# adaLN products on unsplit fp32 weights, four 512-column strips in the array's four column groups, with 8 KB rows per load

## What is computed

```python
def adaln(c, w, b):
    mod = jax.nn.silu(c) @ w + b                 # (sequences, 2048) @ (2048, 6144)
    shift, scale, gate = jnp.split(mod[:, None, :], 3, axis=-1)
    return shift, scale, gate

for l in range(2):                               # 0: windowed attention, 1: mLSTM
    h = rmsnorm(x, g_pre[l]) * (1.0 + scale) + shift
    y = branch_l(h)                              # in-projection, mixer, SiLU gate, out-projection
    x = x + gate * rmsnorm(y, g_post[l])
```

## Time and profile before

| | |
|---|---|
| median of 3 runs | 2599.01 us (2595.3 to 2606.03) |
| span of the profiled execution | 2596.8 us |
| PE busy | 2449.3 us, 94% |
| weight loads of PE (beside its matmuls) | 2259.8 us, 87% |
| VectorE busy | 1213.0 us, 47% |
| ScalarE busy | 875.6 us, 34% |
| mean granted TensorE clock | 0.951 of 2.4 GHz |
| DMA, mean over the span | 116 GB/s |
| loads of w_ada | 32 of 1 MB in ada0, 128 of 0.5 MB in out0 and out1 |

### The profile page before, as it was taken

One profiled execution on the slowest core, in us unless ns is written; L12 is line 12 of the kernel. 1 busy time (PEld: TensorE's weight loads), 2 busy tenths in 40 slices (PEclk: granted clock), 3 DMA queues, 4 the chain that ended last, 5 costly groups with the idle time before them and its releaser, 6 DMA issues.

```text
span 2596.8 us, 42451 instructions
## 1 busy us (share of the span) xinstructions
PE 2449.3 (94%) x17089; PEld 2259.8 (87%) x17089; DVE 1213.0 (47%) x1739; ACT 875.6 (34%) x1303; POOL 65.2 (3%) x108
## 2 busy tenths in 40 slices
PE   5979999999999899999699999999999999989996
PEld 4679989889898598888499999999999999988996
DVE  6663453543544645553943343333343434355424
ACT  5732342332432445553431222121212222234322
POOL 1000000000000000000000000000000000000000
PEclk9989999999999599999899989899999999989998
DMA  8863222222121047777254966774649556616731
GB/s 324 306 211 94 76 55 64 71 66 85 50 68 49 1 151 234 238 242 223 76 111 68 83 85 96 68 98 74 98 66 88 95 88 76 96 50 211 247 81 69
DMA packets 346795, 300.84 MB, mean 116 GB/s; under 512 B 9585, under 2 KB 288361, under 8 KB 345497
## 3 DMA queue, kind: packets, MB, share of 16 engines
q1 hardware_dynamic: 336976, 247.88, 44.9%
q0 software_dynamic: 9360, 50.19, 5.3%
q10 hardware_dynamic: 290, 0.27, 0.0%
HBM read 274.81 MB, written 27.56 MB: 116 GB/s over the span
## 4 chain that ended last, share of the span: by engine, by line
PE 82%; DMA 7%; DVE 5%; ACT 3%; issue 2%; DVEq 1%; ACTq 0%; SPq 0%
PE PJ L746 57%; DMA arena<-in_w_ada 3%; PE MX L938 3%; PE MX L864 3%; PE MX L885 3%; DMA raw<-in_w_in_mlstm 3%; PE PJ L711 2%; PE MX L871 2%; PE MX L1060 1%; PE MX L1070 1%; DMA raw<-in_w_in_attn 1%; PE MX L828 1%; PE MX L1022 1%; DVE strips L1788 1%; DMA obuf<-in_w_ada 1%
## 5 line engine op out<-in xcount | busy, mean ns | idle before, releaser
L746 PE MATMUL PJ<-h_hi,w_hi 128*128 128x272 f32 x4384 | 944.3, 297 | 39.0 <-DVE h_lo L1579 24.7
L746 PE MATMUL PJ<-h_hi,w_lo 128*128 128x272 f32 x4384 | 922.1, 292 | 0.0
L746 PE MATMUL PJ<-h_lo,w_hi 128*128 128x272 f32 x4384 | 920.9, 292 | 0.1
L746 PEld LDWEIGHTS PJ<-h_hi,w_hi 128*128 128x128 f32 x4384 | 713.8, 193 | 73.6 <-issue 38.6
L746 PEld LDWEIGHTS PJ<-h_lo,w_hi 128*128 128x128 f32 x4384 | 705.8, 193 | 0.0
L746 PEld LDWEIGHTS PJ<-h_hi,w_lo 128*128 128x128 f32 x4384 | 701.3, 193 | 0.2 <-issue 0.2
L1521 DVE TENSOR_TENSOR w_lo<-raw,w_hi 128x2048 fp32r<-128x2048 f32 x106 | 242.9, 2292 | 406.5 <-ACT w_hi L1159 406.4
L1159 ACT ACTIVATE w_hi<-raw 128x2048 fp32r<-128x2048 f32 x106 | 202.0, 1905 | 42.1 <-DMA raw<-in_w_in_mlstm 34.6
L1788 DVE TENSOR_TENSOR strips<-arena,strips 128x1024 fp32r<-128x1024 f32 x128 | 153.1, 1223 | 82.2 <-ACT strips L1349 80.4
L1349 ACT ACTIVATE strips<-arena 128x1024 fp32r<-128x1024 f32 x128 | 131.4, 1060 | 107.9 <-DMA arena<-in_w_ada 107.5
L938 PE MATMUL MX<-strips,cT 128*128 128x512 f32 x512 | 141.9, 399 | 17.9 <-DVE strips L1788 17.9
(11 more groups left out here) (303 smaller groups left out, 2137.1 us busy)
## 6 DMA issues: line engine op xcount, KB each, us to landing
arena<-in_w_ada SPq DMA_DIRECT2D x128, 512.0 KB, 5.0
raw<-in_w_in_mlstm SPq DMA_DIRECT2D x64, 1024.0 KB, 14.8
raw<-in_w_in_attn SPq DMA_DIRECT2D x40, 1024.0 KB, 5.6
obuf<-in_w_ada SPq DMA_DIRECT2D x32, 1024.0 KB, 7.8
raw<-in_w_out_attn SPq DMA_DIRECT2D x16, 1024.0 KB, 7.8
raw<-in_w_out_mlstm SPq DMA_DIRECT2D x16, 1024.0 KB, 6.5
x_spill<-arena POOLq DMA_DIRECT2D x2, 4352.0 KB, 12.3
arena<-x_spill POOLq DMA_DIRECT2D x2, 4352.0 KB, 17.7
```

Source lines behind the costliest of these rows:

```text
L746: last = mm(PJ[:, 2 * pair + f, 0:HT], w, h[:, k, HT * f:HT * f + HT], start=(k == 0 and n == 0), stop=(k == KT - 1 and n == 2))
```

## The change

- Nothing of the adaLN weights is split any more. A step takes 128 rows x 2048 columns in full fp32: four products with the same 32 columns of c (nine real ones and the next row block's or padding), each 512 moving columns into 32 partitions of one PSUM bank, thus into its own quarter of the array's columns (`ada_step`). Six quads of 2048 columns take 16 steps each, instead of 24 groups.
- Loads are 1 MB with rows of 8 KB, in four buffers: obuf in the first stage, the arena later.
- First stage: no phase of its own in the table of weight units. 32 steps alternate between shift and scale, PE waits only for the load, and a buffer is free after its step. The turns of x lie behind steps 2, 4, ..., 10 and one row block of square sums behind each of steps 14 to 29. SP no longer waits for c.
- out0 and out1: four steps per block, behind row blocks 4, 7, 10 and 13, in the same blocks as before. SP issues the four loads of block k-1 ahead of the weight of block k.
- A finished quad (4 x 32 partitions x 512) is copied by ScalarE and turned by four 128 x 128 transposes, in the next block behind row block 3; VectorE adds the bias, which is loaded once at the start (bvec, a fourth small load that `vec_in` waits for) and turned with the norm weights. POOL issues no bias loads and waits for no group: its spill of x waits for the turned x only.
- The loops of out0 and out1 over pairs of blocks are written out.

```diff
-OWNER = dict(A="d", Z="d", O="d", Q="a", K="a", V="a", Y="a", G="a")
+OWNER = dict(Z="d", O="d", Q="a", K="a", V="a", Y="a", G="a")
 L0K = "VQQQQKZZZZ"
 L1K = "QKVVZOZO"
-PHASES = [("ada0", 1, "A" * 8), ("l0", GR, L0K), ("out0", 1, "Y" * KT), ("gate", 1, "G"),
-          ("l1", MH, L1K), ("out1", 1, "Y" * KT)]
+PHASES = [("l0", GR, L0K), ("out0", 1, "Y" * KT), ("gate", 1, "G"), ("l1", MH, L1K), ("out1", 1, "Y" * KT)]
 
...
-SEGS = dict(out0=[(0, 2, None), (2, 4, (0, 2 * D, 8)), (6, 8, (1, 0, 12))],
-            out1=[(0, 2, None), (2, 4, (1, 2 * D, 20)), (6, 8, None)])
-SQ_PARTS = {(5, 3): range(0, 4), (5, 7): range(4, 8), (6, 3): range(8, 12), (6, 7): range(12, KT)}
-STRIPS = 8
-RING = 4
+ADA = 4
+QUADS = dict(out0=(2, 3, 4), out1=(5,))
+STEPS = {"out0": {2 + s // 4: range(4 * (s // 4), 4 * (s // 4) + 4) for s in range(0, 48, 4)},
+         "out1": {2 + s // 4: range(48 + 4 * (s // 4), 48 + 4 * (s // 4) + 4) for s in range(0, 16, 4)}}
+QCOL = {2: (0, 2 * D), 3: (1, 0), 4: (1, D), 5: (1, 2 * D)}
+X_TURN = {2: 0, 4: 1, 6: 2, 8: 3, 10: 4}
+SQ_AT = {14 + k: k for k in range(KT)}
...
-            sp.wait_ge(c_in, 32)
-            for u in range(32):
-                if u >= 4:
-                    sp.wait_ge(lo_done, 2 * (u - 3))
-                if u == 28:
+            for u in range(2 * KT):
+                if u >= ADA:
+                    sp.wait_ge(a0_used, u - ADA + 1)
+                if u == 2 * KT - 2:
 
                     sp.wait_ge(xt_done, 5)
                     for e in range(2):
                         load_entry((None, 0), e)
-                slot = obuf[:, 4 * (u % 4):4 * (u % 4) + 4, 0:512]
-                sp.dma_start(slot, ada[:, 0, 4 * (u % 4):4 * (u % 4) + 4,
-                                       512 * (u // 4):512 * (u // 4) + 512]).then_inc(a0_in[u % 4], 16)
+                sp.dma_start(a0_raw[u % ADA], ada[:, 0, u // 2, D * (u % 2):D * (u % 2) + D]).then_inc(a0_in[u % ADA], 16)
...
+                for k in range(1, KT + 1):
+                    if k - 1 in STEPS[ph]:
+                        for s in STEPS[ph][k - 1]:
+                            l, col = QCOL[2 + s // KT]
+                            if s == STEPS[ph][2][0]:
+                                for se, v in arena_free:
+                                    sp.wait_ge(se, v)
+                            if s >= ADA:
+                                sp.wait_ge(u_used, s - ADA + 1)
+                            sp.dma_start(u_raw[s % ADA], ada[:, l, s % KT, col:col + D]).then_inc(u_in[s % ADA], 16)
+                    if k < KT:
+                        load(ph, (None, 0), k, 0, w[:, :, P * k:P * k + P])
...
-            out_units("out0", wout[0], [(kv_stored, 32 + 64 * GR)])
+            out_units("out0", wout[0], [(kv_stored, 32 + 64 * GR), (om_done, 1 + 18 * GR)])
-                if t:
-                    bias(t - 1, t == 1)
-                bias(a)
-            bias(8)
-            pool.wait_ge(u_used, RING + 12 * STRIPS)
+            pool.wait_ge(u_used, 3 * KT)
-                bias(a)
...
-            def ada_products(ph, it, e, mid=None):
-
-                pair = pair_of(ph, e)
-                for j in range(8):
-                    s = j // 2 % 2
-                    pe.wait_ge(lo_done, unit_no(ph, it, e, j) + 1)
-                    for k in range(2):
-                        lhsT = cT[:, (2 * j + k) * 18:(2 * j + k) * 18 + P]
-                        at = SW * (j % 2) + k * 512
-                        for w in (w_hi, w_lo):
-                            last = mm(PJ[:, 2 * pair, :], lhsT, w[s][:, at:at + 512],
-                                      start=(j == 0 and k == 0 and w is w_hi),
-                                      stop=(j == 7 and k == 1 and w is w_lo))
-                    last.then_inc(w_used, 1)
-                    if mid:
-                        mid(j)
-
-            def ada_turn(ph, it, e, n):
-
-                pair = pair_of(ph, e)
-                pe.wait_ge(mod_copied, n + 1)
-                pe.wait_ge(bias_in, n * 16 + 16)
+            def ada_step(bank, weights, k):
+
+                lhsT = cT[:, NSEQ * k:NSEQ * k + 32]
+                for g in range(4):
+                    last = mm(bank[32 * g:32 * g + 32, :], lhsT, weights[:, 512 * g:512 * g + 512],
+                              start=(k == 0), stop=(k == KT - 1))
+                return last
+
+            def ada_turn(bank, rows_):
                 for j in range(4):
-                    last = mm(PJ[:, 2 * pair + 1, 9 * j:9 * j + 9], misc[32:51, P * j:P * j + P],
-                              fix[32:51, C_SEL:C_SEL + NSEQ], start=True, stop=True)
+                    last = tr(bank[:, P * j:P * j + P], rows_[:, P * j:P * j + P], ident)
                 last.then_inc(mod_turned, 1)
...
+            for u in range(2 * KT):
+                pe.wait_ge(a0_in[u % ADA], 16 * (u // ADA + 1))
+                ada_step(PJ[:, u % 2, :], a0_raw[u % ADA], u // 2).then_inc(a0_used, 1)
+                if u in X_TURN:
+                    turn_x(X_TURN[u])
+                if u in SQ_AT:
+                    sums(0, [SQ_AT[u]])
+            for q in range(2):
+                pe.wait_ge(mod_copied, q + 1)
+                ada_turn(PJ[:, 2 + q, :], mod_rows[q])
...
-            def strip(n, j):
-
-                at = fixed(pe, n + 1)
+            def strip(s):
+
                 pe.wait_ge(ct_ready, 1)
-                pe.wait_ge(u_lo_done, at)
-                for k in range(2):
-                    lhsT = cT[:, (2 * j + k) * 18:(2 * j + k) * 18 + P]
-                    for w in (u_hi, u_lo):
-                        last = mm(MX[:, 2, :], lhsT, w[j % RING][:, k * 512:k * 512 + 512],
-                                  start=(j == 0 and k == 0 and w is u_hi),
-                                  stop=(j == STRIPS - 1 and k == 1 and w is u_lo))
-                last.then_inc(u_used, 1)
-
-            def turn_group(n):
-
-                pe.wait_ge(ct_ready, 1)
+                pe.wait_ge(u_in[s % ADA], 16 * (s // ADA + 1))
+                ada_step(MX[:, 2, :], u_raw[s % ADA], s % KT).then_inc(u_used, 1)
+
+            def turn_quad(n):
+
                 pe.wait_ge(mod_copied, n + 1)
-                pe.wait_ge(bias_in, n * 16 + 16)
-                pe.wait_ge(mod_taken, n - 7)
-                for j in range(4):
-                    last = mm(MX[:, 3, 9 * j:9 * j + 9], misc[32:51, P * j:P * j + P],
-                              fix[32:51, C_SEL:C_SEL + NSEQ], start=True, stop=True)
-                last.then_inc(mod_turned, 1)
+                pe.wait_ge(mod_taken, n)
+                ada_turn(MX[:, 3, :], mod_rows[0])
...
+                for k in range(KT):
+                    if k >= 2:
+                        pe.wait_ge(*freed_at(ph, it0, k - 2))
+                    pe.wait_ge(lo_done, UNIT0[ph] + k + 1)
+                    points = dict(extra) if k == 0 else {}
+                    if k in STEPS[ph]:
+                        points = {4 + 3 * i: (lambda s=s: strip(s)) for i, s in enumerate(STEPS[ph][k])}
+                    if k - 1 in STEPS[ph] and (k - 2) % 4 == 0:
+                        points[3] = lambda n=2 + STEPS[ph][k - 1][-1] // KT: turn_quad(n)
+                    block(slot_of(ph, k), pair_of(ph, k), points, h_base if k == 0 else None)
...
+            act.dma_start(bvec, b_ada.rearrange("l (k p) -> (l k) p", p=P)).then_inc(vec_in, 16)
...
-            def mod_copy(ph, e, n, it):
-
-                act.wait_ge(w_used, ended(ph, it, e))
-                if ph != "ada0" or n:
+            def mod_copy(bank, rows_, used, n, sem_):
+
+                act.wait_ge(sem_, used)
+                if n > 2:
                     act.wait_ge(mod_turned, n)
-                fn(misc[32:50, 0:512], PJ[0:18, 2 * pair_of(ph, e), :], ACT.Copy).then_inc(mod_copied, 1)
+                fn(rows_, bank, ACT.Copy).then_inc(mod_copied, 1)
...
+            for t in range(5):
+                n = P if t < 4 else TS
+                act.wait_ge(xt_done, t + 1)
+                act.wait_ge(ct_ready, 1)
+                for b in range(2):
+                    fn(xw[:, 4 * b:4 * b + 4, P * t:P * t + n],
+                       MX[:, b, 0:4 * n].rearrange("p (k t) -> p k t", k=4), ACT.Copy).then_inc(xe_a, 1)
+            act.wait_ge(xe_a, 10)
+            act.wait_ge(xe_d, 10)
+            squares(0)
+            root(1)
+            for q in range(2):
+                mod_copy(PJ[:, q, :], mod_rows[q], 2 * KT - 1 + q, q, a0_used)
...
-                            for j in range(STRIPS):
-                                if j == RING:
-                                    ahead(k, r)
-                                landed = 16 * (2 * (g - 8) + j // RING + 1)
-                                act.wait_ge(u_in[j % RING], r * 64 + landed)
-                                fn(u_hi[j % RING], u_raw[j % RING], ACT.Copy).then_inc(u_hi_done, 1)
-                            act.wait_ge(u_used, r * (2 * STRIPS) + (RING + STRIPS * (g - 7)))
```

(16 more changed lines are left out.)

299 lines of the change are left out of this document (76 added, 223 removed).

## The result

The changed kernel takes 2566.06 us (median of 4 runs, 2560.8 to 2575.33) where the kernel before, on the same chip, takes 2600.89 (4 runs, 2595.3 to 2606.03): a ratio of 0.9882, 95% interval 0.9860 to 0.9903. The profiled execution spans 2559.3 us where before it was 2596.8. So 37.5 us went (34.8 between the medians), where the forecast said 99.5: it is faster, as forecast, but the gain is a little over a third of the one forecast, and the time lies just above the range.

A forecast was written before the change was run, and what follows sets the result against it. PE, busy 94% of 2596.8 us, was taken as the bound, with loads bounding the start. Savings of 63 + 22 + 14.5 = 99.5 us gave a span of 2497.3; with 2.2 added, the forecast was 2499, range 2480 to 2516.

The forecast's parts named there:

- The step, 1.15 us: adaLN step on PE: four fp32 products in separate column groups overlap, 1.15 us including switches, bounds 0.86 and 3.65.
- two at a time: Rival for the adaLN step: only two column groups run together, 2.0 us a step, 2558 us in all; chance 0.17.
- program order: Rival for the adaLN step: matmuls start strictly in order, 2.45 us with switches, 2591 us, no change; chance 0.05.
- one after another: Rival for the adaLN step: the four groups run singly, 3.65 us a step, 2703 us in all; chance 0.08.
- Blocks of out0 and out1, 16.9 us, 63 and 22: Blocks with adaLN steps fall to 16.9 us from 22.18 (out0) and 22.35 (out1), saving 63 and 22 us.
- Loads stay hidden, share near 0.85: out0 and out1: loads need 14.2 of a block's 16.9 us, so stay covered; DMA share near 0.85 in out0.
- Loads lead: Rival: mixed DMA rate below 310 GB/s paces out0; at 276 GB/s, 34 us given back, 2533 us; chance 0.10.
- Start, 14.5: First stage, bound by loads: first use of the modulation at 123.5 instead of 138.06, 14.5 us saved, bounds 5 and 27.
- l1 at nothing: Stage after the first use of the modulation, l1 included, was to keep its length; no term for l1.

The follow-up runs named there:

- a_onegroup: Changed kernel with all four products of a step sent to one column group from the second step of each quad on; 2752.34 us, ratio 1.060.
- a_2kb: Changed kernel with each adaLN load of 8 KB rows cut into four loads of 2 KB rows; 2578.91 us, ratio 0.9924.
- a_start3: Changed kernel with c turned first, first two l0 weights issued after the last adaLN loads, sinks' eight loads replaced by VectorE copies; 2565.56 us, ratio 0.988.
- b_room3143: Kernel before the change with an unused input of 12.9 MB (3143 pages) declared ahead of the others; forecast to lose 50 us, lost 14.
- a_room449: Changed kernel with 449 pages of unused input declared ahead of the others, a repeat with more rounds; 2525.8 us.
- d449: Changed kernel with an unused input of 1839104 bytes (449 pages) declared ahead of the others, first run; 2524.62 us, ratio 0.9711.
- a_all: a_start3 with 449 pages of unused input declared ahead of the weights; 2511.13 us, ratio 0.9668 to the kernel before the change.
- b_pad7: Kernel before the change with seven unused columns (3584 bytes) added behind the constants; 2596.94 us, ratio 1.000.
- a_start: Changed kernel with PE turning c first and the g and bias rows only after the second step; 2574.65 us, ratio 0.9919.

## Why the prediction was right or wrong

**The step, 1.15 us: right.** Four groups at once, 0.99 us on PE and 1.18 with the way back to full-width products. The out-of-order start read in the earlier trace rows holds: first passes of all groups come before the second pass of the first. The Trainium skill's rule of a start in program order ("TensorE: Matmul & The Clock Gate", Part 3) would have had 2.45 us here by the prediction's estimate; it does not hold for L828 and L829 of the earlier trace rows, nor for these passes if the two of a product stand together in the program, which no run shows. Its 4 ns between starts on different tiles does roughly, 6 to 7 ns here. The rivals two at a time, program order and one after another are out, the last shown by a_onegroup.

**Blocks of out0 and out1, 16.9 us, 63 and 22: right,** 16.88 and 16.81, 62.5 and 22.3. The turn and the copy ahead of it cost 0.44 us every fourth block, no handoff on the path.

**Loads stay hidden, share near 0.85: right in effect, the size off.** The share was 0.92 at 292 GB/s, and a_2kb has the same with 2 KB rows. My 10.6 us for four loads at 396 GB/s was too optimistic for mixed rows, and a block of 16.9 has little left. "Loads lead" did not happen.

**Start, 14.5: mechanism right, three terms wrong; 6.5 came.** (1) The sum has the buffers nearly full at 20.5 us and 408 GB/s from there on. They were nearly full (three had landed at 18.0, the fourth at 23.3), but while the sinks' loads landed, up to 28 us, the engines moved 45 GB/s, 8 us that I had not asked for. In before the stretch ahead of the forecast's full stream is nearly empty too, and I took that for the wait for c alone. (2) The two l0 weights are issued ahead of the last two adaLN loads, and SyncE's queue stood there for 9 us; I had summed their bytes and not their place. (3) The last step ran at a granted clock of 0.50 (1.2 GHz), behind a wait for its load, and took 1.98 us, not 1.1. Against that the full stretches ran faster than the 408 GB/s taken (426 from 60 to 90 us, above). Mending (1) and (2), with c turned first as well (a_start3), brought 20.0 us over before at block 0, inside the bounds of 5 and 27. The limit of about 358 GB/s for a core that the Trainium skill's "DMA: Bandwidth & Descriptors" gives under Specifications did not bind here: 426 GB/s over 30 us.

**l1 at nothing: the step that failed.** The sum has no term for l1, since no line of it changes ("The stage from there on keeps its length"), and l1 lost 53.8 us, against which the 8 us short at the start are small. What I could have read: the earlier trace rows don't show it, but in the trace of before some l1 loads take 21 us with the engines full at 64 GB/s, and PE stands still for only 9.6 us of l1 by luck of their place. Had I asked how near these loads are to PE, I should have carried "another layout exposes them, up to some 50 us" as a case. With the layout of before's pattern the changed kernel takes 2525.8, and with the start mended 2511.1, 12 us from the forecast of 2499: its l1 is 16.1 us longer than before's (1037.4 against 1021.3), its start 5.1 better than the sum had (19.6 us for 14.5). That this comes near the forecast does not make the forecast right: it had neither the l1 term nor these two changes.

**Left open.** What moves the weights between the two families. It is not the constants, the spill tensor, the number of adaLN transfers, or 262144 bytes of input; 1839104 bytes of input do it. The program itself is a candidate that was not tried. Nor is it known what makes b_room3143's loads less slow at the same offsets, or why with the slow loads at 1536 and 3584 l1 takes 1034 to 1038 us in the changed kernel (a_room449, d449, a_all) and 1021 to 1027 in before and b_pad7. That the place of the weights in DRAM is the cause at all rests on runs that add nothing but an unused input, and on the slow columns moving by the bytes computed in four of five of them; no address was read, each pattern is that of one profiled execution, and the mechanism behind is open. The nearest rule is in the Trainium skill's "DMA: Bandwidth & Descriptors", Latency and other measured facts: copies between DRAM tensors with rows at a pitch of 4 MiB run at half the rate of those at 512 KiB, and 4 KiB of padding restores it. Here the 16 rows of a partition are 4 MiB and 8 KiB apart and partitions 32832 bytes, and the loads are slow for some column offsets only, down to 46 GB/s. No run here varied the pitch.

## What to carry to other kernels

Small fp32 products with at most 32 outputs each belong in different column groups of the array: four at once took 0.99 us here, and one after another 3.55. Before a stage that the change does not touch is put at nothing, ask which of its loads are near the edge: a DMA share near 1 at a low GB/s is the row to look for, and compare the same load in two kernels before blaming the code. Look for loads of single elements ahead of a stage that DMA bounds, and at where bulk issues of short rows stand in a queue, not only at their bytes.

## What was not expected of the hardware

- One 1 MB load of 512-byte rows takes 11.3 us or 22.8 us by what is declared ahead of its tensor and its column offset, at a DMA share of 0.77 and of 0.99 (packets of 62 and 176 ns), and this repeats load by load in kernels with the same pattern.
- Eight loads of 0.5 KB made of 4-byte elements leave the engines at a share of 0.12 to 0.17 for 8 us, in a_start while adaLN loads of 1 MB stand in the queue beside them.
- An unused input of 1.8 MB ahead of the weights makes this program some 40 us faster, one of 3.7 MB some 25, one of 0.26 MB does nothing.
